# Inverse roots of the last stage: square root and reciprocal, or logarithm and exponential

## What is computed

```python
def rwkv_output(y, feats, r_k, ln_w, ln_b, w_out):
    ...
    mean = jnp.mean(y, axis=-1, keepdims=True)
    var = jnp.mean(jnp.square(y - mean), axis=-1, keepdims=True)
    yn = ((y - mean) * lax.rsqrt(var + GN_EPS)).reshape(b_, t, D_INNER).astype(gz.dtype) * ln_w + ln_b
    ...
    return ((yn + bonus.reshape(b_, t, D_INNER)) * jax.nn.silu(gz)) @ w_out
...
    x = x + gt * rmsnorm(o_lat, norm_post[i])
```

## Time and profile before

| | |
|---|---|
| time before, median of 3 runs | 2535.53 us (2534.56 to 2537.11) |
| the profiled execution | 2540.85 us, span 2539.0 us |
| mean granted TensorE clock | 0.969 of full speed |
| busy over the span: PE, DVE, ACT, POOL | 2309.0, 1140.9, 780.4, 623.8 us |
| last stage | from about 2356 us to the end of the span |

### The profile page before, as it was taken

How to read it: one execution, slowest core, us unless ns; L and a number is a source line. 1 busy time by engine, 2 the same in 40 slices (tenths; PEclk the granted TensorE clock), 3 DMA queues, 4 the chain that set the end, 5 groups by cost and what they waited for, 6 DMA issues and landing times. The chain is left out here.

```text
span 2539.0 us, 56698 instructions
## 1 busy us (share of the span) xinstructions
PE 2309.0 (91%) x24172; PEld 1455.8 (57%) x24172; DVE 1140.9 (45%) x2235; ACT 780.4 (31%) x1992; POOL 623.8 (25%) x913
## 2 busy tenths in 40 slices
PE   7999999999969997999997798989899898988598
PEld 3555555534534443544443677777777777777354
DVE  4111111112374675021220566666666666665684
ACT  4000000013314551220000344444444444454221
POOL 0000000001212331000000444444454444443243
PEclk9999999999979998999999799999999999999699
DMA  9200000150002765455422234333333333331542
GB/s 366 118 17 25 17 21 21 67 199 25 34 35 72 200 191 157 146 153 172 166 91 88 76 94 149 88 92 88 91 83 95 83 92 85 91 88 49 189 125 87
DMA packets 296667, 261.95 MB, mean 103 GB/s; under 512 B 105440, under 2 KB 255200, under 8 KB 293856
## 3 DMA queue, kind: packets, MB, share of 16 engines
q1 hardware_dynamic: 296416, 258.32, 32.9%
HBM read 178.54 MB, written 79.69 MB: 102 GB/s over the span
## 5 line engine op out<-in xcount | busy, mean ns | idle before, releaser
L770 PE MATMUL ps<-xt,w_slab 128*128 128x512 f32 (+1 forms) x1376 | 551.4, 557 | 28.8 <-DMA w_slab<-in_w 18.9
L770 PEld LDWEIGHTS ps<-xt,w_slab 128*128 128x128 f32 x1376 | 260.3, 192 | 315.2 <-issue 263.6
L363 PE MATMUL ps<-h,fw_slab 128*128 128x512 f32 (+1 forms) x768 | 278.1, 524 | 2.1 <-ACT h L250 2.1
L1676 PE MATMUL ps<-M,AT 64*64 64x64 f32 x6400 | 270.9, 224 | 4.8 <-DVE M L1576 2.0
L1439 POOL TENSOR_TENSOR SP<-Q,decay 64x128 f32<-64x128 f32 x304 | 138.1, 454 | 464.1 <-DVE Q L1616 434.9
L1676 PEld LDWEIGHTS ps<-M,AT 64*64 64x64 f32 x6400 | 220.0, 135 | 48.4 <-issue 14.6
L1676 PE MATMUL ps<-TT,MT 64*64 64x64 f32 x5120 | 216.8, 224 | 18.5 <-ACT XT L1501 15.3
L363 PEld LDWEIGHTS ps<-h,fw_slab 128*128 128x128 f32 x768 | 146.4, 191 | 132.4 <-issue 124.1
L1676 PEld LDWEIGHTS ps<-TT,MT 64*64 64x64 f32 x5120 | 178.2, 135 | 49.4 <-issue 38.2
L1562 DVE COPY_PREDICATED TT<-mask,ps 128x256 f32<-128x256 int32 x400 | 166.8, 435 | 75.9 <-PE ps L1676 73.1
L532 POOL TENSOR_TENSOR xt<-scaled_out,xt 128x1024 f32<-128x1024 f32 x10 | 23.5, 2348 | 666.2 <-DVE scaled_out L565 666.2
(11 more groups left out here) (195 smaller groups left out, 3101.0 us busy)
## 6 DMA issues: line engine op xcount, KB each, us to landing
feat<-feature_scratch SPq DMA_DIRECT2D x160, 256.0 KB, 3.0
feature_scratch<-k_feats SPq DMA_DIRECT2D x64, 320.0 KB, 5.1
w_slab<-in_rwin SPq DMA_DIRECT2D x32, 512.0 KB, 5.9
feature_scratch<-k_feats SPq DMA_DIRECT2D x24, 640.0 KB, 6.9
mod_slab<-in_modw SPq DMA_DIRECT2D x8, 1536.0 KB, 6.6
Q<-v_token_scratch SPq DMA_DIRECT2D x320, 32.0 KB, 2.5
Z<-v_token_scratch SPq DMA_DIRECT2D x320, 32.0 KB, 2.3
fgo<-in_modw SPq DMA_DIRECT2D x8, 1024.0 KB, 9.7
```

Of the source, the lines that this page charges most:

```text
L363: mm = pe.matmul(ps[:, b0 + b, 0:n], wi[:, half, k, :], h0[:, k, a:a + n], start=k == 0, stop=k == KT - 1)
L770: mm = pe.matmul(ps[:, bank, 0:n], w[:, i % 2, k, :], src[:, k, a:a + n], start=k == 0, stop=k == KT - 1)
L1676: mm = pe.matmul(out[o, b, :], L[o, b, :], R[o, b, :], start=True, stop=True)
```

## The change

The root and its reciprocal are replaced by a logarithm and an exponential, `exp(-0.5 * ln(v + eps))`, both on ScalarE, for the 32 items of the group norm and for the 8 tiles of the row norm. VectorE's two reciprocals go. Between the logarithm and the exponential ScalarE waits for its own semaphore. The semaphore that lets PE reuse a variance bank now counts logarithms.

```diff
                     def var(i):
                         pe.wait_ge(sq_ready, i + 1)
                         if i >= 2:
-                            pe.wait_ge(root, i - 1)
+                            pe.wait_ge(log, i - 1)
...
-                            act.activation(sd[(s - 1) % 2][:], ps[:, 2 + (s - 1) % 2, 0:QT], ACT.Sqrt, scale=1.0 / HD, bias=eps[:, 1:2]).then_inc(root, 1)
+                            act.activation(sd[(s - 1) % 2][:], ps[:, 2 + (s - 1) % 2, 0:QT], ACT.Ln, scale=1.0 / HD, bias=eps[:, 1:2]).then_inc(log, 1)
+                            act.wait_ge(log, s)
+                            act.activation(sd[(s - 1) % 2][:], sd[(s - 1) % 2][:], ACT.Exp, scale=-0.5).then_inc(inv, 1)
...
-                            act.activation(rs[:, t:t + 1], ss[:, t:t + 1], ACT.Sqrt, scale=1.0 / D, bias=eps[:, 0:1]).then_inc(o_root, 1)
+                            act.activation(rs[:, t:t + 1], ss[:, t:t + 1], ACT.Ln, scale=1.0 / D, bias=eps[:, 0:1]).then_inc(o_log, 1)
+                            act.wait_ge(o_log, t + 1)
+                            act.activation(rs[:, t:t + 1], rs[:, t:t + 1], ACT.Exp, scale=-0.5).then_inc(o_inv, 1)
...
-                        v.wait_ge(root, i + 1)
-                        v.reciprocal(sd[i % 2][:], sd[i % 2][:]).then_inc(inv, 1)
                         v.wait_ge(inv, i + 1)
...
-                            v.wait_ge(o_root, t + 1)
-                            v.reciprocal(rs[:, t:t + 1], rs[:, t:t + 1]).then_inc(o_inv, 1)
                             v.wait_ge(o_inv, t + 1)
```

More of the change, by code:

```diff
@@ L1086, in build @@
             y_in, b_in, g_in = ([sem(f"{n}{r}") for r in ring] for n in ("y_in", "bonus_in", "gate_in"))
-            x_in, y_sum, mean_mm, centred, sq_ready, var_mm, root, inv, normed, biased, gated = (sem(n) for n in (
-                "last_x1_in", "y_sum", "mean_mm", "centred", "y_sq_ready", "var_mm", "y_root", "y_inv", "y_normed", "y_biased", "gated"))
+            x_in, y_sum, mean_mm, centred, sq_ready, var_mm, log, inv, normed, biased, gated = (sem(n) for n in (
+                "last_x1_in", "y_sum", "mean_mm", "centred", "y_sq_ready", "var_mm", "y_log", "y_inv", "y_normed", "y_biased", "gated"))
             scaled = sem("y_scaled")
-            pd_ready, pb_mm, pb_out, o_mm, o_ss, o_root, o_inv, o_used, res, st = (sem(n) for n in (
-                "last_post_diag_ready", "last_post_rows_mm", "last_post_rows_out", "out1_mm", "out1_sum", "out1_root", "out1_inv", "out1_used", "result_ready", "out_stored"))
+            pd_ready, pb_mm, pb_out, o_mm, o_ss, o_log, o_inv, o_used, res, st = (sem(n) for n in (
+                "last_post_diag_ready", "last_post_rows_mm", "last_post_rows_out", "out1_mm", "out1_sum", "out1_log", "out1_inv", "out1_used", "result_ready", "out_stored"))
             oband = lambda t: ps[:, 4 + 2 * (t % 2):6 + 2 * (t % 2), :].rearrange("p b t -> p (b t)")
```

## The result

The changed kernel takes 2558.3 us (median of 20 runs) against 2535.8 for the kernel before on the same chips: ratio 1.0082, 95% interval 1.007 to 1.0093, that is +20.8 us (17.8 to 23.6). The two medians are 22.5 us apart; the ratio is one of means, and a single run of the kernel before at 2559.9 us makes most of that difference. The forecast was slower, 2550.8 (+15.3), with a range of 2528 to 2556. The direction and the mechanism held, the size did not: it was 5.5 us short by the ratio, and the median lies 2.3 us above the range.

The account below looks back on a forecast made before the run. The last stage was taken as bound first by DVE's reciprocal and the x1 load, then by PE. Terms 0.8 + 13.1 - 1.2 + 2.6 = +15.3 on 2535.5 gave 2550.8 us, range 2528 to 2556.

Parts of the forecast that it names:

- second phase: Last stage, 2410 to 2497, PE busy throughout: ScalarE's table loads make it the bound, +13.1 us from item 13 to 31.
- gate of item 31: Last item, from its root to its projection: 5.63 us now, 4.45 after the change, -1.2 us.
- deciding step: Last stage's table loads: one at each change between Ln and Exp, 80 in all, where one stood; chance 0.54.
- estimate of 2620: Whole kernel at the skill's 2.66 us per switch: 80 us more over the items, 5 in the tail; not used.
- First phase: Last stage, 2364 to 2400, before projections: ScalarE's loop 3.82 us against DVE's 3.36, first projection 0.8 us later.
- 19.7 for four steps: Second phase: time per four steps, from ScalarE's 19.4 us against PE's 17.2, taking PE's order into account.
- Tail: Last tile, root to scaling: two exposed loads, Ln and Exp take 3.16 us where 0.53 was, +2.6 us.
- One load with the full gain: Rival: one load serves Ln and Exp, x1 load starts 3.5 us earlier; -5.25 us, 2530.3; chance 0.28.
- One load with the small gain: Rival: one load, but the x1 transfer isn't started usefully earlier; -1.8 us, 2533.8; chance 0.13.
- Loads hidden by PE: Rival: loads at each change, absorbed by PE's lead over ScalarE; +2.2 us, 2537.7; chance 0.05, others of that size included.

Follow-up runs that it names:

- shared-set kernel: Changed kernel with one table load, of a set holding Ln and Exp, heading ScalarE's last stage; 0.9982 of the kernel before, -4.6 us.
- tiles-only kernel: Kernel before with Ln and Exp for the eight tiles alone, items keeping root and reciprocal; 1.0036 of the kernel before, +9.1 us.

## Why the prediction was right in kind and short in size

The mechanism held, and the time fell outside the range because two terms of the sum were mis-sized: the second phase (+13.1, measured +15.9) and the gate of item 31 (-1.2, measured +0.4).

**The deciding step** was that Ln and Exp would each get a load. It was read from the pattern of 24 loads, and the trace after has all 80. That Ln would follow the pattern was a judgement at even odds (0.54), not something that the rows showed. The Trainium skill (ScalarE: Activation LUTs, Table sets: the hidden batching unit) is right that a set with both exists, since the shared-set kernel ran both from one load; its count of one load for ln then exp did not come true here, where the set must be named by hand. The Trainium skill's price of 2.66 us for a switch (ScalarE: Activation LUTs, What ACT_TABLE_LOAD costs) is not what this kernel pays: 1.29 us from 2420.29 to the ACTIVATE at 2421.58. My estimate of 2620 by that price was also low: in the forecast's own loops 1.36 us more for each load makes 6.54 us of an item and 152 us of the 18 steps, 75 over before there alone.

**First phase, +0.8.** Right: 3.82 us from Ln to Ln, forecast 3.82, and +0.8 at the first projection. One premise was too wide: that a load starts without waiting for its ACTIVATE's semaphore holds only where it stands ahead of the wait, as the one before an item's Ln does here.

**Second phase, "+13.1".** This is the term that failed: right in kind, 2.8 short. The 18 intervals are five with a tile, 39.7 us (7.95 each, forecast 7.97), eight of 3.82 (30.6), and five paced by PE (22.5). Those five are where I was short: 4.3 us where my 19.7 for four steps left 4.1, and one of 5.33 where PE fell to half clock behind a wait of 2.38 us for the square. In that stretch four steps took 21.4 us and not 19.9.

```profile
2440.00:2460.00 20.00, 17.62 (x45) 9.03 (x44) 8.15 (x16) 18.22 (x26) 7.36 (x8) 0.91 0.36 105
...
2500.00:2520.00 20.00, 17.19 (x40) 8.11 (x40) 6.97 (x13) 15.24 (x22) 5.25 (x5) 0.91 0.38 147
```

The wait of 2.38 us before 2430.30, just as long, was followed by no fall (1.00 from 2420 to 2440), so where the clock falls could not have been told from these rows. I had named it as a risk and left it out of the sum. Half a microsecond is an error of mine: step 32 has no mean, so before it was 76.9 and not 77.4.

**Gate of item 31, "-1.2".** Wrong, +0.4. I let PE wait for the last gate as soon as item 31's Ln was done, and forgot what was queued on PE itself: twelve more projection records, 5.2 us at full clock. The gate ended 5.4 us after that Ln (2518.00), later than forecast (4.45), since the multiply by the inverse root took 1.41 us beside POOL's work. PE did not wait for it, because the clock had fallen to half again behind the last square (0.50 from 2512.6 to 2514, and a mean of 0.91 in the second row above), so that the twelve records took longer than that. The 76 records took 34.0 us where the shared set's take 32.8. At full clock 0.8 us were to be gained, which the shared set shows (32.58 us from item 31's Ln to the end of the projections, against 33.36 before), and the clock took 1.2.

**Tail, +2.6.** Right: 4.30 against 1.71 us from the end of the projections to the last scaling.

The terms come to +20.0 measured against +15.3 forecast: 2.8 in the second phase, 1.6 at the gate, 0.3 of clock at the first projections (from the first of them to the next mean 5.94 us and not 5.66). About 1.5 of the second phase's and 1.2 of the gate's are the clock, so roughly 3 of the 4.7 us. The range's upper end allowed 5.2 us for the clock alone and nothing for an error in a term. What is not settled is whether the other 19 runs have the same shares, since only one was profiled: the medians are 22.5 us apart, the profiled stages 20.0.

**Rivals.** One load with the full gain: true of the shared set, false of the change. Its -3.5 does not follow from its own loop of 2.55 us, by which item 2 is normalised at 2372.0 and not 2371.4 (-2.9); measured was -3.2, of which 1.0 was lost again by the later landing. One load with the small gain: false, the x1 load did start and land earlier. Loads hidden by PE: false here, nearly true once a tile's functions stood beside an item's, and not true of the tiles-only kernel, although its demand was far under PE's.

## What to carry to other kernels

Count an engine's demand per period of the loop, with its table loads, against the engine that sets the pace: below it 70 loads cost 2 us, above it 80 cost 21. Then look at what stands behind the loads in the same queue. With ScalarE half idle, 22 loads cost 9 us, because they stood in front of an item's root. Before moving a function to ScalarE, read from the trace whether its neighbours share a load, and if a shared set exists, load it by name ahead of the first wait. When a stage is sped up, look for the bulk transfer in its queue: here it withheld nearly half of the gain.

## What the runs showed of the hardware

In all these traces a table load took 1283 ns, and it runs in program order. Ahead of a wait it hides behind another engine's work (0.44 us from the square's start to the load); behind the wait it adds its full length (1.72 us to the load, and then the load).

VectorE's multiply by the inverse root grew from a mean of 476 to 594 ns in the changed kernel. The traces show where: it takes 0.42 or 0.43 us whenever no elementwise instruction of POOL runs beside it (27 of 32 before, 24 of 32 after). The others overlap one of POOL's and take 0.68 to 1.01 us before and 0.56 to 1.43 after, longer by a third to nine tenths of the time for which the two overlap.

```profile
L1236 DVE TENSOR_TENSOR y_centred<-y_centred,y_std 128x256 f32<-128x256 f32 x32 | 19.0, 594 | 86.4 <-ACT y_std L1187 86.4
...
2513.66 2.34 POOL L1228 TENSOR_TENSOR x<-last_scaled_out,x 128x1024 f32<-128x1024 f32 x1 [0.47 <-DVE last_scaled_out L1256]
...
2514.87 1.41 DVE L1236 TENSOR_TENSOR y_centred<-y_centred,y_std 128x256 f32<-128x256 f32 x1 [1.29 <-ACT y_std L1187]
```
